# Moving the depthwise-convolution sums into PSUM, and reordering the first and the last chunk of a fused encoder block

## The chip, the cores and the metric

The kernel runs on one core of a Trainium2 chip. The metric is the device time of one execution in microseconds; lower is better. The time before is the median of three executions.

## The reference

One hybrid residual block over a sequence of 2048 positions with 1024 features, in fp32. Cut to what matters:

```python
u = rms_norm(h, g_pre_mix)
z = u @ w_in                                   # [GLU a, b | q | k | v | gates A, B]
c = a * sigmoid(b)
c = causal_depthwise_conv(c, conv_dw_w, conv_dw_b)          # 31 taps, 512 channels
y_conv = silu(layer_norm(c, conv_ln_g, conv_ln_b)) @ w_conv_out
y_attn = sliding_window_sink_attention(rope(q), rope(k), v, sinks) @ w_attn_out
h = h + rms_norm((sigmoid(gA) * y_conv + sigmoid(gB) * y_attn) @ w_out, g_post_mix)

gate, val = split(rms_norm(h, g_pre_ffn) @ w_up)            # 2 x 2816
gate = causal_depthwise_conv(gate, ffn_dw_w, ffn_dw_b)      # 3 taps
h = h + rms_norm((gelu(gate) * val) @ w_down, g_post_ffn)
h = h + (p @ w_ple) * sigmoid(h @ w_ple_gate)
```

## The kernel before

The sequence is cut into four chunks of 512 positions. Inside a chunk every activation lies feature-major: tiles of 128 features by 512 positions. Every fp32 product is made of three single-pass matmuls (`w_hi*x_hi`, `w_hi*x_lo`, `w_lo*x_hi`, lines 748 to 750, or 772, 773 and 776 where several output tiles advance together), so all activations that feed TensorE are split into a rounded part (ScalarE writes it) and the rest (VectorE subtracts).

**The weights** come as 122 blocks of eight 128x128 tiles, 512 KB each, through three slots, in the order that `block_order` writes out. In chunk 0 each block is fresh: SyncE loads it into `w_stage`, GpSimd casts it to `w_hi` (line 416) and subtracts four times to `w_lo` (line 419), and SyncE stores both halves to DRAM. Chunks 1 to 3 load the two stored halves and leave GpSimd idle. A slot is loaded again when TensorE has finished with its block (`block_done`). A block is 24 matmuls of 512 columns.

**The stages of a chunk on TensorE**: four GLU pairs; q, k, v; attention in four steps, each with two gate-A blocks, the transposes of the probabilities, the next scores and the product with v; the merge (eight gate-B blocks, four attention-out blocks, four convolution-out blocks, interleaved); `w_out`, between whose blocks the next chunk's input and the residual rows are transposed; the feed-forward in three groups of up blocks (8, 8 and 6 feature tiles, each a gate half and a value half) and a down product; the per-layer embedding. For chunks 1 to 3 the GLU pairs stand between `w_out` and the feed-forward of the chunk before, and q, k, v behind that feed-forward.

**The convolution** is VectorE work: `tap(j)` adds one of 31 taps of channel tile j into `conv_acc` in SBUF with one 128x512 instruction (line 1225), 124 taps a chunk. For chunk 0, `EARLY` = 15 taps of tiles 0 and 1 are made before `glu(0, 2)`, 15 taps of tiles 2 and 3 between the rotations (`rope`), and the remaining 64 in the four attention steps, 16 in each; then come `ln_sum`, `ln_centre`, the LayerNorm and only then the merge. For later chunks the taps stand among the up tiles of the chunk before, six to a tile and 40 in a row (`taps(40)`) beside the first down product. The mean of the LayerNorm is a matmul with ones (line 928), the token sums are matmuls with one column (line 785), and the inverse roots are spread over partitions by a matmul with a diagonal (line 792) into PSUM bank 7 (`BC`); bank 6 (`SMALL`) takes the sums.

All synchronisation is written by hand: each engine runs its own list in order and waits on counters such as `glu_done`, `merged`, `y2_out`, `v_out`, `ft_ready`. TensorE waits for `y2_out` of `w_out` tile 1 (line 1038) ahead of each of the last four `w_out` blocks. ScalarE makes `attend_q(0, 0)`, which waits for all rotations, ahead of `value_out(0)`. In the last chunk, which has no next GLU to run in between, the two norms around the residual (POST and PRE) stand one behind the other (lines 1064 to 1067) ahead of the first up blocks.

## Time and profile before

| | |
|---|---|
| median of 3 executions | 3052.34 us (3048.07 to 3063.79) |
| the profiled execution's own time | 3061.3 us |
| its span on the profile | 3059.5 us |
| mean granted TensorE clock | 0.976 |
| TensorE busy (matmuls) | 2885.7 us, 94% |
| VectorE busy | 1424.3 us, 47% |
| ScalarE busy | 805.5 us, 26% |
| GpSimd busy | 581.3 us, 19% |
| chain that ended last | TensorE 81%, VectorE 9%, GpSimd 4%, DMA 3% |

Each execution of the profile has start times counted from the beginning of its span. A busy TensorE is a matmul in flight, not TensorE at its peak; the clock column (1.00 is 2.4 GHz, 0.50 is 1.2 GHz) says how fast it was allowed to run. The chunks are told apart on TensorE's timeline by the operands: the first scores of chunk 0 start at 143.8 us and those of chunks 1, 2 and 3 at 951.9, 1668.4 and 2382.9 us.

### The profile page before, as it was taken

The page shows a single profiled execution, that of the slowest core. Times are in us where ns is not written, and L with a number is a line of the kernel's source. Part 1 is how long each engine was busy: PE and PEld are TensorE (multiplying, and loading weights), DVE is VectorE, ACT ScalarE, POOL GpSimd, SP SyncE. Part 2 cuts the span into 40 slices and gives each one's busy share as a digit, 9 for nine tenths or more (in the row PEclk, how much of TensorE's full clock was granted, in tenths as well). Part 3 has the DMA queues.
Part 4 walks back from the last instruction along what each step waited for, and adds up shares of the span by engine and source line. Part 5 has one row for each costly group of instructions (what it writes and reads, how often), then busy time and mean ns, then how long its engine had stood idle before and what let it go on. Part 6 is the DMA issues. An engine that isn't in the chain of part 4 may idle for free.

```text
span 3059.5 us, 33182 instructions
## 1 busy us (share of the span) xinstructions
PE 2885.7 (94%) x13080; PEld 2377.3 (78%) x13080; DVE 1424.3 (47%) x2392; ACT 805.5 (26%) x1539; POOL 581.3 (19%) x614
## 2 busy tenths in 40 slices
PE   6688998798999999999999999999999998899998
PEld 5576787576778888888888888888788886688886
DVE  5885359483354225674343324666325422412124
ACT  2252321111135223211224513211114512211012
POOL 5645638786643000000000000000000000000000
PEclk9799999899999999999999999999999999899999
DMA  5446857576765554555454464555455455355553
GB/s 201 169 152 246 292 205 271 184 269 232 261 223 211 203 212 176 204 193 189 173 190 179 165 240 173 197 192 195 179 186 191 159 188 190 132 194 194 189 192 138
DMA packets 182747, 606.38 MB, mean 198 GB/s; under 512 B 18752, under 2 KB 37440, under 8 KB 182592
## 3 DMA queue, kind: packets, MB, share of 16 engines
q1 hardware_dynamic: 165696, 595.86, 53.6%
q10 hardware_dynamic: 16896, 8.39, 0.9%
q8 instruction: 104, 1.70, 0.2%
q14 instruction: 51, 0.42, 0.0%
HBM read 467.87 MB, written 136.31 MB: 197 GB/s over the span
## 4 chain that ended last, share of the span: by engine, by line
PE 81%; DVE 9%; POOL 4%; DMA 3%; issue 1%; ACT 1%; SPq 0%; DVEq 0%; ACTq 0%
PE ps L748 21%; PE ps L750 21%; PE ps L749 21%; PE ps L772 4%; PE ps L773 4%; PE ps L776 4%; DVE conv_acc L1225 4%; DMA w_stage<-in_weights 3%; POOL w_lo L419 3%; POOL w_hi L416 2%; PE ps L797 1%; PE ps L885 1%; DVE h_tmp L1382 1%; DVE h L1387 1%; PE ps L792 1%
## 5 line engine op out<-in xcount | busy, mean ns | idle before, releaser
L748 PE MATMUL ps<-y_hi,w_hi 128*128 128x512 f32 x1536 | 606.1, 395 | 13.5 <-issue 6.6
L749 PE MATMUL ps<-y_lo,w_hi 128*128 128x512 f32 x1536 | 600.4, 391 | 0.0
L750 PE MATMUL ps<-y_hi,w_lo 128*128 128x512 f32 x1536 | 600.3, 391 | 0.0
L419 POOL TENSOR_TENSOR w_lo<-w_stage,w_hi 128x256 fp32r<-128x256 f32 x488 | 422.9, 897 | 9.8
L1225 DVE SCALAR_TENSOR_TENSOR conv_acc<-conv_in,col,conv_acc 128x512 f32<-128x512 f32 x480 | 396.4, 883 | 0.1
L748 PE MATMUL ps<-f_hi,w_hi 128*128 128x512 f32 x768 | 308.6, 402 | 46.1 <-POOL w_lo L419 36.7
L748 PEld LDWEIGHTS ps<-y_hi,w_hi 128*128 128x128 f32 x1536 | 289.8, 189 | 79.1 <-issue 15.7
L750 PEld LDWEIGHTS ps<-y_hi,w_lo 128*128 128x128 f32 x1536 | 289.9, 189 | 60.9
L749 PEld LDWEIGHTS ps<-y_lo,w_hi 128*128 128x128 f32 x1536 | 290.1, 189 | 59.6 <-issue 0.7
L749 PE MATMUL ps<-f_lo,w_hi 128*128 128x512 f32 x768 | 303.7, 395 | 0.0
L750 PE MATMUL ps<-f_hi,w_lo 128*128 128x512 f32 x768 | 303.0, 395 | 0.0
L748 PE MATMUL ps<-u_hi,w_hi 128*128 128x512 f32 x704 | 281.0, 399 | 3.0 <-DVE conv_in L1245 2.0
L749 PE MATMUL ps<-u_lo,w_hi 128*128 128x512 f32 x704 | 275.6, 391 | 0.0
L750 PE MATMUL ps<-u_hi,w_lo 128*128 128x512 f32 x704 | 275.6, 391 | 0.0
L1415 DVE SCALAR_TENSOR_TENSOR g_conv<-ps,col,g_conv 128x511 f32<-128x511 f32 x88 | 65.8, 748 | 364.3 <-ACT g_conv L589 364.1
L416 POOL CAST w_hi<-w_stage 128x1024 fp32r<-128x1024 f32 x122 | 159.6, 1308 | 354.2 <-DMA w_stage<-in_weights 353.9
L748 PEld LDWEIGHTS ps<-f_hi,w_hi 128*128 128x128 f32 x768 | 146.9, 191 | 87.6 <-issue 35.0
L750 PEld LDWEIGHTS ps<-f_hi,w_lo 128*128 128x128 f32 x768 | 147.0, 191 | 31.6
L749 PEld LDWEIGHTS ps<-f_lo,w_hi 128*128 128x128 f32 x768 | 147.2, 192 | 31.0 <-issue 1.0
L589 ACT ACTIVATE g_conv<-ps,col 128x512 f32<-128x512 f32 x88 | 68.5, 778 | 346.5 <-PE ps L750 284.3
L748 PEld LDWEIGHTS ps<-u_hi,w_hi 128*128 128x128 f32 x704 | 133.4, 189 | 32.9 <-issue 3.7
L1438 DVE TENSOR_TENSOR acc<-acc,ps 128x512 f32<-128x512 f32 x64 | 43.8, 686 | 245.2 <-PE ps L750 245.2
(180 smaller groups left out, 3961.2 us busy)
## 6 DMA issues: line engine op xcount, KB each, us to landing
w_hi<-split_weights SPq DMA_DIRECT2D x366, 512.0 KB, 3.2
w_lo<-split_weights SPq DMA_DIRECT2D x366, 512.0 KB, 4.2
w_stage<-in_weights SPq DMA_DIRECT2D x122, 512.0 KB, 4.5
split_weights<-w_hi SPq DMA_DIRECT2D x122, 512.0 KB, 2.8
split_weights<-w_lo SPq DMA_DIRECT2D x122, 512.0 KB, 4.0
rows_u<-in_x SPq DMA_DIRECT2D x16, 512.0 KB, 5.8
rows_h<-in_x SPq DMA_DIRECT2D x16, 512.0 KB, 6.1
out_h<-o_rows ACTq DMA_DIRECT2D x24, 256.0 KB, 2.8
```

Of the source, the lines that this page charges most:

```text
L416: nc.gpsimd.tensor_copy(w_hi[:, slot], w_stage[:, slot]).then_inc(w_hi_ready, 1)
L419: last = nc.gpsimd.tensor_tensor(w_lo[:, slot, k:k + 2], w_stage[:, slot, k:k + 2], w_hi[:, slot, k:k + 2].bitcast(F32), ALU.subtract)
L589: copy(g_conv[:, t % 2], ps[:, up_bank(t)[0]], ACT.Identity, bias=column("ffn_b", t), scale=column("ffn_w", 3 * t + 2)).then_inc(tap0_read ...
L748: nc.tensor.matmul(bank, w_hi[:, slot, kk], hi, start=start, stop=False)
L749: nc.tensor.matmul(bank, w_hi[:, slot, kk], lo, start=False, stop=False)
L750: return nc.tensor.matmul(bank, w_lo[:, slot, kk], hi, start=False, stop=stop)
L772: nc.tensor.matmul(ps[:, banks[o]], w_hi[:, slot, first + o], hi[:, k], start=(k == 0), stop=False)
L773: nc.tensor.matmul(ps[:, banks[o]], w_lo[:, slot, first + o], hi[:, k], start=False, stop=False)
L776: last = nc.tensor.matmul(ps[:, banks[o]], w_hi[:, slot, first + o], lo[:, k], start=False, stop=(k == 7))
L1225: V.scalar_tensor_tensor(dst, src, column("conv_w", t + j * TAPS), dst, ALU.mult, ALU.add).then_inc(conv_tap, 1)
L1415: V.scalar_tensor_tensor(g_conv[:, n, 1:T], gate[:, 0:T - 1], column("ffn_w", 3 * t + 1), g_conv[:, n, 1:T], ALU.mult, ALU.add).then_inc(t ...
L1438: V.tensor_tensor(acc[:, j], acc[:, j], ps[:, dn_bank(q, j)], ALU.add).then_inc(dn_acc, 1)
```

## The change

The parts, by stage:

- **Input of chunk 0.** VectorE scales two of the four row tiles and ScalarE the other two; the transposes take four PSUM banks in turn (`xu_bank`) in place of two.
- **Taps.** The running sum of `tap(j)` stands in PSUM bank 6 or 7 (`CONV_BANK`), read and written by the same instruction; one tap moves it to `conv_acc`. In chunk 0 that is tap 15 of tiles 0 and 1 and tap 7 of tiles 2 and 3, and the taps after it are in SBUF as before, because attention uses the banks. In later chunks it is the last tap, and tiles 0 and 1 are finished before tiles 2 and 3 begin.
- **Chunk 0.** 32 taps stand ahead of `glu(0, 2)`, 16 among the rotations with each rotation ahead of its four taps, nine in each attention step (36), and 40 in the merge. The merge of chunk 0 has its own block order (`FIRST_MERGE`): gate-B and attention-out blocks first, all four convolution-out blocks last. `merge_attention` puts the attention part into `h`, `merge_conv` adds the convolution part. SyncE loads the next input rows two or three blocks later. `value_out(0)` stands ahead of `attend_q(0, 0)`.
- **`w_out`.** The wait for `y2_out` moves from ahead of each block to ahead of the transposes inside it.
- **LayerNorm of the next chunk.** Its token sums and their spreading move from behind the second down product to inside up tiles 17 and 19.
- **Last chunk.** `h_split` rounds `h * g_pre_ffn`, without the inverse root, for the up product, which takes each tile as it comes. The inverse root is kept in `r_last`, and VectorE multiplies each gate and value result by it in PSUM (two more 128x512 instructions for each of the 22 tiles). The PRE sums stand behind the first two up tiles, the spreading inside the third.
- **Output of the last chunk.** Output tiles 0 to 3 are transposed between the last gate blocks in place of behind them.

```diff
+FIRST_MERGE = [b for i in range(4) for b in (GB_BLOCK[2 * i], GB_BLOCK[2 * i + 1], AT_BLOCK[i])] + CV_BLOCK
...
+        def xu_bank(c, f):
+            return 0 if c else f % 4
...
-                if c + 1 < CHUNKS and 0 <= b - (B_MRG + 9) < TT:
+                rows_with = (CV_BLOCK[2], CV_BLOCK[3], B_WO, B_WO + 1) if c == 0 else range(B_MRG + 9, B_MRG + 9 + TT)
+                if c + 1 < CHUNKS and b in rows_with:
                     sp.wait_ge(silu_ready, (c + 1) * NC)
...
+            def h_split(c, j):
+                act.wait_ge(h_mid, c * KD_ + j + 1)
+                copy(y_hi[:, j], h[:, j], ACT.Identity, bias=0.0, scale=column("g_pre_ffn", j)).then_inc(u2_hi, 1)
...
-            attend_q(0, 0)
             value_out(0)
+            attend_q(0, 0)
...
+                if c == 0:
+                    for i in range(KD_ // 2):
+                        gate_b_block(c, 2 * i)
+                        gate_b_block(c, 2 * i + 1, between=(None, None, lambda: conv_mean(0), lambda: spread(LN, 0))[i])
+                        attention_outs(c, i)
+                        if i == 2:
+                            token_sums(LN, 0)
+                    for i in range(KD_ // 2):
+                        conv_outs(c, i)
...
-                    pe.wait_ge(y2_out, c * KD_ + 2)
                     def turns(f):
+                        pe.wait_ge(y2_out, c * KD_ + 2)
...
-                    token_sums(PRE, c)
-                    spread(PRE, c)
...
+                if not more:
+                    token_sums(PRE, c)
                 for t in range(2, FB[1]):
-                    up(c, t)
+                    up(c, t, between=(lambda: spread(PRE, c)) if not more and t == 2 else None)
...
-                if more:
-                    token_sums(LN, c + 1)
...
+                    if more and t == FB[2] + 1:
+                        up(c, t, between=lambda: token_sums(LN, c + 1))
+                    elif more and t == FB[2] + 3:
+                        up(c, t, between=lambda: spread(LN, c + 1))
...
                 src = conv_in[:, j, ds(t, T)]
-                dst = conv_acc[:, j]
+                last = TAPS - 1 if conv_chunk[0] else (EARLY, EARLY, EARLY // 2, EARLY // 2)[j]
+                dst = ps[:, CONV_BANK[j % 2]] if t < last else conv_acc[:, j]
+                old = ps[:, CONV_BANK[j % 2]] if t <= last else conv_acc[:, j]
...
-                    V.scalar_tensor_tensor(dst, src, column("conv_w", t + j * TAPS), dst, ALU.mult,
+                    V.scalar_tensor_tensor(dst, src, column("conv_w", t + j * TAPS), old, ALU.mult,
                                            ALU.add).then_inc(conv_tap, 1)
...
-                    taps(6 if more else LATE)
+                    taps(4)
...
+                if c + 1 == CHUNKS:
+                    done(c, up_done(t, 0))
+                    V.tensor_tensor(gate, gate, r_last[:, :], ALU.mult).then_inc(gate_scaled, 1)
...
+                    V.tensor_tensor(val, val, r_last[:, :], ALU.mult).then_inc(val_scaled, 1)
...
                 if c == 0:
+                    taps(12)
+                    merge_attention(0)
+                    taps(14)
+                    merge_attention(1)
+                    taps(14)
                     ln_sum(0)
```

## Rows read from the trace of the kernel before

**Rows 1.** The page: busy time, share of span and instructions of each engine.

```profile
PE 2885.7 (94%) x13080; PEld 2377.3 (78%) x13080; DVE 1424.3 (47%) x2392; ACT 805.5 (26%) x1539; POOL 581.3 (19%) x614
```

**Rows 2.** Waits of TensorE, whole span: us in total, times, longest us.

```profile
PE ps L748 <- POOL w_lo L419: 43.2, 17, 22.0
PE ps L827 <- ACT v_feat L480: 25.4, 1, 25.4
PE ps L785 <- DVE ssum L1177: 23.0, 6, 15.5
PE ps L797 <- DVE rows_u L1182: 21.5, 1, 21.5
PE ps L874 <- DVE prob L1310: 8.7, 4, 4.8
```

**Rows 3.** Stages of chunks 0 and 1: busy by engine, clock, DMA share, GB/s.

```profile
143.80:227.40 83.60, 74.67 (x386) 65.06 (x385) 70.97 (x123) 44.94 (x139) 34.68 (x34) 0.87 0.40 138
227.40:331.10 103.70, 93.38 (x399) 74.34 (x399) 48.51 (x66) 22.36 (x36) 66.28 (x77) 0.97 0.69 250
331.10:951.90 620.80, 570.25 (x2472) 462.24 (x2470) 348.64 (x490) 147.51 (x230) 393.12 (x415) 0.96 0.67 243
...
951.90:1020.30 68.40, 68.40 (x417) 60.63 (x416) 27.83 (x78) 43.55 (x136) 0.00 (x0) 1.00 0.47 161
1020.30:1107.50 87.20, 87.20 (x388) 72.19 (x387) 17.45 (x28) 10.19 (x20) 0.00 (x0) 1.00 0.59 214
1107.50:1668.40 560.90, 555.38 (x2471) 456.48 (x2470) 278.07 (x490) 147.65 (x230) 0.00 (x0) 0.99 0.52 189
```

**Rows 4.** Trains of taps on VectorE's timeline: start, us, instruction.

```profile
60.93 32.18 DVE L1225 SCALAR_TENSOR_TENSOR conv_acc<-conv_in,col,conv_acc 128x512 f32<-128x512 f32 x28
...
549.41 17.97 DVE L1225 SCALAR_TENSOR_TENSOR conv_acc<-conv_in,col,conv_acc 128x512 f32<-128x512 f32 x27
```

**Rows 5.** GpSimd's timeline beside trains of taps, and just behind one.

```profile
69.34 4.50 POOL L419 TENSOR_TENSOR w_lo<-w_stage,w_hi 128x256 fp32r<-128x256 f32 x4
...
547.33 20.96 POOL L416 CAST w_hi<-w_stage 128x1024 fp32r<-128x1024 f32 x1 [9.82 <-DMA w_stage<-in_weights]
...
572.18 2.79 POOL L419 TENSOR_TENSOR w_lo<-w_stage,w_hi 128x256 fp32r<-128x256 f32 x4
```

**Rows 6.** VectorE with PSUM operands, GpSimd at work: ns min/median/max; one instruction.

```profile
L1415 DVE SCALAR_TENSOR_TENSOR g_conv<-ps,col,g_conv x8: 736/737/749, 457.0 to 522.1; 128x511 f32<-128x511 f32 x8
...
147.31 0.43 DVE L1293 TENSOR_TENSOR ps<-ps,prev_bias 128x256 f32<-128x256 f32 x1 [6.87 <-PE ps L841]
```

**Rows 7.** Start of chunk 0: ScalarE, then TensorE.

```profile
23.45 0.69 ACT L454 ACTIVATE u_hi<-ps,col 128x512 fp32r<-128x512 f32 x1 [0.17 <-PE ps L797]
...
33.19 0.80 PE L772 MATMUL ps<-u_hi,w_hi 128*128 128x512 f32 x1 [1.56 <-DVE u_lo L1186]
...
142.86 1.11 PE L827 MATMUL ps<-ident,v_feat 128*128 128x128 f32 x4 [25.44 <-ACT v_feat L480]
```

**Rows 8.** First down product of chunk 0 and 1, third up group, first up group.

```profile
530.70:600.30 69.60, 47.51 (x192) 38.45 (x193) 36.27 (x54) 4.19 (x7) 49.07 (x37) 0.83 0.47 173
...
763.40:817.80 54.40, 54.40 (x240) 44.68 (x238) 19.91 (x33) 10.09 (x15) 39.64 (x51) 1.00 0.78 289
...
1209.40:1296.70 87.30, 87.30 (x386) 72.27 (x386) 54.83 (x100) 19.71 (x29) 0.00 (x0) 1.00 0.55 202
1296.70:1340.30 43.60, 43.59 (x192) 35.77 (x191) 36.17 (x58) 4.82 (x8) 0.00 (x0) 1.00 0.53 193
```

**Rows 9.** TensorE in chunk 1: inside `w_out`, and behind the second down product.

```profile
1131.59 0.77 PE L748 MATMUL ps<-y_hi,w_hi 128*128 128x512 f32 x1 [2.20 <-issue]
...
1474.39 1.05 PE L785 MATMUL ps<-ones,ssum 128*128 128x1 f32 x8 [1.45 <-DVE ssum L1177]
```

**Rows 10.** Last chunk: from the last `w_out` block to the up blocks; the tail.

```profile
2588.40:2618.80 30.40, 7.09 (x21) 3.75 (x20) 21.80 (x47) 9.12 (x16) 0.00 (x0) 0.56 0.09 35
...
3047.60:3059.50 11.90, 4.77 (x33) 3.16 (x31) 6.44 (x10) 0.60 (x1) 0.00 (x0) 0.87 0.62 176
```

More of the change, by code:

```diff
@@ L620, in _ @@
             x_norm(0)
+            act.wait_ge(norm_step, 6)
+            for t in range(TT // 2, TT):
+                copy(rows_u[:, t], rows_u[:, t], ACT.Identity, bias=0.0, scale=n_r[:, t:t + 1]).then_inc(x_scaled, 1)
             for f in range(KD_):
@@ L728, in _ @@
                     ple_gate(c, j)
-            for f in range(KD_):
-                store_rows(CHUNKS - 1, f, o_last)
+                    if not more and j >= 5:
+                        store_rows(c, 2 * j - 10, o_last)
+                        store_rows(c, 2 * j - 9, o_last)
+            store_rows(CHUNKS - 1, 6, o_last)
+            store_rows(CHUNKS - 1, 7, o_last)
             act.wait_ge(out_stored, CHUNKS * 16 * KD_)
@@ L937, in up @@
                     full_block(c, up_block(t) + half, up_bank(t)[half], y_hi, y_lo)
+                    if half == 0 and between is not None:
+                        between()
             def down(c, q, between=None):
@@ L1119, in _ @@
                 ple_gate(c, 5)
+                if not more:
+                    out_tile(c, 0, PG_BANK[0])
+                    out_tile(c, 1, PG_BANK[1])
                 pe.wait_ge(ple_out, c * KD_ + KD_)
                 ple_gate(c, 6)
+                if not more:
+                    out_tile(c, 2, PG_BANK[0])
+                    out_tile(c, 3, PG_BANK[1])
                 pe.wait_ge(h3_step, (c + 1) * KD_)
@@ L1124, in _ @@
                 if not more:
-                    for f in range(KD_):
-                        out_tile(c, f, 6 + f % 2)
+                    for f in range(4, KD_):
+                        out_tile(c, f, PG_BANK[f % 2])
         @block.vector
@@ L1231, in taps @@
                 for _ in range(n):
-                    j = min(range(NC), key=lambda j: next_tap[j])
+                    pair = (0, 1) if conv_chunk[0] and next_tap[1] < TAPS else (2, 3) if conv_chunk[0] else range(NC)
+                    j = min(pair, key=lambda j: next_tap[j])
                     if next_tap[j] < TAPS:
@@ L1318, in attend @@
                         out_rows(c - 1, f, OT + f % 2, o_rows)
-                if c == 0 and more:
-                    taps(4)
+                if c == 0:
+                    taps(3)
                 for s in range(2):
@@ L1327, in attend @@
                                     ALU.subtract).then_inc(ao_lo, 1)
-                if c == 0 and more:
-                    taps(LATE - 10)
+                if c == 0:
+                    taps(2)
             def ln_sum(c):
@@ L1470, in _ @@
             dve.wait_ge(glu_done, 2)
-            for t in range(EARLY):
+            for t in range(EARLY + 1):
                 tap(0)
@@ L1478, in _ @@
             for j in range(PAIRS + 1):
-                for t in range(min(EARLY, 4 * j), min(EARLY, 4 * j + 4)):
-                    tap(2)
-                    tap(3)
                 if j == PAIRS:
@@ L1484, in _ @@
                 rope(0, j)
+                if j < PAIRS:
+                    for n in range(4):
+                        tap(2 + n % 2)
             for c in range(CHUNKS):
@@ L1497, in _ @@
                     ln_rest(0, 0, NC)
-                for i in range(KD_ // 2):
-                    merge(c, i)
+                    merge_attention(3)
+                    for i in range(KD_ // 2):
+                        merge_conv(i)
+                else:
+                    for i in range(KD_ // 2):
+                        merge(c, i)
                 zero_sum()
@@ L1525, in _ @@
                         residual(c, j - 1, mid_step, h_mid)
+                    if not more and j >= 1:
+                        h_rest(c, j - 1)
                     if j >= 2:
@@ L1535, in _ @@
                     glu(c + 1, 2)
+                    dve.wait_ge(bc_ready, SUM_AT[PRE, c] + 1)
+                    dve.wait_ge(h_mid, (c + 1) * KD_)
+                    for j in range(KD_ + 1):
+                        if j < KD_:
+                            u2_tile(c, j)
+                        if j >= 1:
+                            u2_rest(c, j - 1)
+                    glu(c + 1, 3)
+                    glu_keep(c + 1)
                 else:
                     zero_sum()
-                dve.wait_ge(bc_ready, SUM_AT[PRE, c] + 1)
-                dve.wait_ge(h_mid, (c + 1) * KD_)
-                for j in range(KD_ + 1):
-                    if j < KD_:
-                        u2_tile(c, j)
-                    if j >= 1:
-                        u2_rest(c, j - 1)
-                if more:
-                    glu(c + 1, 3)
-                    glu_keep(c + 1)
+                    keep_root()
                 for t in range(FB[0], FB[1]):
@@ L1573, in _ @@
                     if more and t == FB[2] + 1:
+                        token_norm(LN, c + 1, CONV)
+                        zero_sum()
+                    if more and t == FB[2] + 3:
                         ln_scale(c + 1)
@@ L1606, in _ @@
                     ple_add(c, j)
-            for f in range(KD_):
-                out_rows(CHUNKS - 1, f, 6 + f % 2, o_last)
+                    if not more:
+                        for f in (2 * j - 8, 2 * j - 7):
+                            out_rows(c, f, PG_BANK[f % 2], o_last)
             dve.wait_ge(root_ready, len(NORM_AT))
```

157 lines of the change are left out of this document (105 added, 52 removed).

## The prediction

> **What bounds the kernel now.** The page says TensorE is in flight 94% of the span [rows 1]; so the gain to be had is its idle time and its slow clock, and the question is where those lie. The list of TensorE's waits names them [rows 2]: 43 us for GpSimd's `w_lo`, one wait of 25 us for `v_feat`, 23 us for token sums (one of 15.5 us), 21.5 us at the start, 9 us for probabilities. The table of stages shows in which chunk: attention takes 83.6 us in chunk 0 and 68.4 us in chunk 1, the merge 103.7 and 87.2, and everything from `w_out` to the next scores 620.8 and 560.9 [rows 3]. Chunks 1 to 3 run at TensorE's own pace (87.2 us for 16 blocks, 5.45 us each, at clock 1.00), so nothing is won there but small waits. The loss is in chunk 0, and in the 30.4 us of the last chunk in which TensorE works 7 us [rows 10].
>
> Why chunk 0 is slow shows when VectorE's trains of taps are laid beside GpSimd's timeline. A tap costs 32.18/28 = 1.15 us while GpSimd works on weights and 17.97/27 = 0.67 us where it does not [rows 4]. GpSimd pays too: four subtractions take 4.50 us beside taps and 2.79 us without, and one cast that came in the middle of `taps(40)` took 20.96 us, until the train was over [rows 5]. That is the 22 us wait of TensorE. A tap reads two SBUF tensors. The instructions of the up tiles that read one operand from PSUM keep 736 to 749 ns while GpSimd works [rows 6]. A tap with its sum in PSUM should do the same.
>
> **The change part by part.** *Price of a tap in PSUM.* No instruction of the trace has the full form (SBUF and PSUM in, PSUM out, 512 wide). The nearest rows are the PSUM-reading one (737 ns in duration, as a free tap) and the one that reads and writes the same PSUM bank, 256 wide in 0.43 us [rows 6], which is 0.16 us plus 256 elements at 0.96 GHz, as for SBUF. So I take 0.67 us. Bounds: not below 0.6, and up to 1.15 if it still meets GpSimd. The Trainium skill, VectorE: DVE Perf Modes, section on the TRN2 errata, speaks against the change: it gives a PSUM source 62 cycles more fixed cost than an SBUF source, by its figures an estimated 65 ns a tap; over the 44 taps before the scores that would take 3 us from the gain, 2928 in place of 2925. The durations of rows 6 do not show it.
>
> *Start.* The first GLU matmul is at 33.19 us [rows 7] and the first transposes at 21.5 [rows 2]. With two of four rows scaled on ScalarE they start about 2.5 us sooner, and with four banks the eight tiles follow at 0.86 us (the start of the second rounding, 23.45, less the first 0.86 before it) in place of pairs at 2.74: 18.9 + 1.1 + 7 x 0.86 + 1.7 for the last two eviction steps = 27.7. Gain 5.5 us.
>
> *To the scores, before at 143.8.* VectorE now does 32 taps in 21.4 us after `glu(0, 1)` (before 33.7), so `glu(0, 2)` and `(0, 3)` are in time for q and k, and TensorE's eight GLU and six q, k, v blocks run through: 27.7 + 46.2 + 33.9 = 107.8. Each rotation (2.0 us) with four taps (2.7) fits in a 5.45 us block, so the key's rotation ends near 109, `value_out` no longer waits for `attend_q`, and the scores start near 110.5. The 25.4 us idle [rows 7] and the slow clock behind it go. Gain so far 33.3 us.
>
> *Attention, before 83.6.* Nine SBUF taps in a step in place of 16. Chunk 1 shows the pace without taps, 68.4 with 2 us of output transposes [rows 3]. VectorE's other work is 6.6 us a step, nine taps at 1.15 add 10.4, against a TensorE step of 16.3: just even. I take 68.3 with 2 us for jitter and clock: gain 15.3. Gate-B starts near 179.
>
> *Merge, before 103.7.* 16 blocks are 87.2 [rows 3]. What is late next is `conv_mean`, which TensorE now issues inside the eighth block, 41 us in. VectorE still has 42 SBUF taps, two pieces of attention merge and three sums: at 1.15 us it is ready some 16 us late, at 0.67 some 5 us late; in the wait GpSimd runs dry and the last taps get cheap, so 12. With 2.5 us of slow clock behind the wait, and 3 us for weights (GpSimd needs 1.5 + 4.5 = 6.0 us for a block beside taps [rows 5], more than TensorE's 5.45; SyncE's queue holds the load of the third convolution block behind `silu_ready`), this stage costs 104.7, nothing won. The moved row loads are covered: the rows are wanted 22 us into `w_out`. `w_out` starts near 283.5: gain 47.6 in all, bounds 38 and 58.
>
> *Rest of chunk 0, before 620.8.* Chunk 1's 560.9 less 6.7 us (next part) is the clean length, 554. To it comes what fresh weights cost even without taps: two blocks must be there at each down product, about 3 us and the clock three times, 6 us before the embedding and 6 us in small waits. So 575. The largest piece is the first down product, 69.6 against 43.6 us [rows 8]. The third up group (54.4 us in chunk 0, no taps beside it) shows that the fresh stream holds TensorE's pace, at 289 GB/s [rows 8]. Gain 45.8, bounds 30 and 57.
>
> *`w_out` and LayerNorm.* TensorE stands 2.2 us for `y2_out` [rows 9], and a slow-clock window behind it doubles some matmuls, another 1.4 us. Moved nine matmuls (2.0 us) further back, the wait is nearly met. The token sums wait 1.45 us [rows 9] and again cost about 1.6 in clock; two up tiles later VectorE has long summed. Gain 6.7 us in each of chunks 1 and 2 (13.4), and 2.1 for `w_out` in chunk 3; chunk 0's share is in its 575.
>
> *Last chunk.* The 30.4 us [rows 10] lose the wait for PRE. The residual tiles start at 2595.8; the first is normed, added, rounded and subtracted by 2599. Then each tile costs VectorE 2.5 us and 0.7 us of waiting for ScalarE's rounding, 3.2, against 2.72 for TensorE's 12 matmuls: the first up product ends near 2622.5 in place of 2642.6. Token sums, spreading, and a stall of 0.7 us at up tile 3, which waits for the first scaled tile, take back 2.8. Gain 17.3, bounds 12 and 20. The 44 scalings are 0.68 us each, hidden: a tile has 10.9 us on TensorE and its chain through VectorE and ScalarE is under 7. Tail: four output tiles earlier, but 2.2 us of their transposes now stand ahead of the last gate: gain 0.7 of 11.9 [rows 10].
>
> **Sum**: 47.6 + 45.8 + 13.4 + 2.1 + 17.3 + 0.7 = 126.9. The profiled execution's own time is 3061.3 (span 3059.5), so 2934.4; the median of the runs is 9.0 below it: 2925.
>
> **The rivals.** *A: the taps in PSUM still collide with GpSimd.* The source is still in SBUF. Against it stand rows 6, of just such mixed operands. Then 32 taps take 36.8 us before `glu(0, 2)`, each rotation step exceeds a block, and the cast can starve: some 15 us of the opening and 35 of the rest are lost, 2975.
>
> *B: the fresh weights bind.* Faster consumption asks for a block every 5.45 us all through chunk 0; a load takes some 5 us and GpSimd 3.9 to 6.0, with only two blocks of cover (10.9). For it: 43 us of waits for `w_lo` now. Against it: the third up group. If half of the FFN gain goes (23) and the merge loses 9 more: 2957.
>
> *C: slower than before.* An instruction that reads and writes one bank at full width might run far slower than the half-wide one of the trace [rows 6]. The first up group of chunk 1 has VectorE busy 54.8 of 87.3 us with 42 taps [rows 8], so a tap can grow by 0.77 us, to 1.44, unseen. There are 252 such taps in three chunks; to eat 127 us each must cost 0.5 more: from about 1.95 us a tap the kernel is slower than before, at 2.0 it takes some 3066.
>
> *D: a long starved cast in the merge.* Trains of 12 and 14 SBUF taps remain; a cast that meets one waits up to 9 us, most of it inside the wait already counted. 2932, within the forecast's own range.
>
> **How the numbers follow.** The forecast 0.74 (with D), A 0.07, B 0.15, C 0.02, and 0.02 for an effect under 15 us. Its own range is the sum of bounds, 2903 to 2952. To leave out no more than 2 in 10 the range reaches to B: 2900 to 2965. What a measurement of this kernel can tell is about 0.5%, 15 us: faster 0.95, same 0.03, slower 0.02.
>
> **What would show it.** In the profile after: taps into PSUM at 0.67 us beside a working GpSimd; no cast over 2 us in the feed-forward; scores of chunk 0 near 110; one wait of TensorE of some 12 us at the mean of the LayerNorm, near 220; the first down product of chunk 0 under 50 us; chunks 1 and 2 at about 710 us each; less than 12 us between the last residual transposes and the first up matmul of chunk 3. It is wrong if waits for `w_lo` stay near 40 us (B), if taps in PSUM take over 0.8 us (A, C), or if VectorE in attention is late and the steps stay near 19 us.

## The result: 3.5% faster, and what the trace after shows

The changed kernel takes 2949.68 us (median of 4 runs, 2943.44 to 2954.17), against 3057.35 us for the kernel before on the same chip (4 runs, 3048.07 to 3063.79). The ratio is 0.9646, 95% interval 0.9625 to 0.9666: 107.7 us less. The forecast was 2925 with a range from 2900 to 2965. The two profiled executions are 3061.3 and 2943.4, 117.9 apart, where the sum of the prediction said 126.9.

The page of the changed kernel, busy time of each engine (answers to [rows 1]):

```profile
PE 2854.6 (97%) x13080; PEld 2358.7 (80%) x13080; DVE 1405.2 (48%) x2427; ACT 807.6 (27%) x1541; POOL 523.2 (18%) x614
```

TensorE has the same 13080 matmuls, but is 31 us less in flight with them: fewer ran at the lower clock (the mean granted clock is 0.991, before 0.976). GpSimd has the same 614 instructions in 523.2 us in place of 581.3, although no edit touches them.

The changed kernel's waits of TensorE (answers to [rows 2]): us in total, times, longest us.

```profile
PE ps L828 <- DVE rows_u L1236: 19.1, 1, 19.1
PE ps L779 <- POOL w_lo L433: 14.1, 10, 2.4
PE ps L964 <- DVE ssum L1397: 13.6, 1, 13.6
```

The 43.2 us for `w_lo` are 14.1, no wait for them is over 2.4 us, and the waits for `v_feat` and `prob` have left the head of the list. One wait has grown, that of the mean of chunk 0's LayerNorm for the channel sum: 13.6 us, where the same matmul stood 7.5 us in the kernel before:

```profile
PE ps L928 <- DVE ssum L1334: 7.5, 1, 7.5
```

The changed kernel by stages (answers to [rows 3], [rows 8] and [rows 10]). Columns: stretch, us, busy time of PE, PEld, DVE, ACT, POOL, granted clock, DMA share, GB/s. They are chunk 0's attention, its merge, the rest up to the next scores; the first down product of chunk 0; chunk 1 whole; the last chunk from its last residual transposes to the first up matmul; its first up product; the last chunk from its scores.

```profile
107.70:176.60 68.90, 68.61 (x385) 60.18 (x385) 51.58 (x101) 45.54 (x141) 34.85 (x39) 0.95 0.53 183
176.60:286.70 110.10, 94.19 (x398) 74.69 (x396) 87.47 (x101) 21.83 (x35) 79.18 (x77) 0.92 0.64 234
286.70:865.20 578.50, 558.18 (x2471) 456.30 (x2472) 314.49 (x490) 148.41 (x231) 342.40 (x415) 0.99 0.72 261
...
478.00:526.10 48.10, 45.97 (x193) 37.23 (x194) 37.55 (x57) 4.19 (x7) 30.25 (x38) 0.96 0.68 256
865.20:1575.50 710.30, 707.58 (x3272) 587.06 (x3271) 324.38 (x596) 201.34 (x385) 0.00 (x0) 1.00 0.53 191
2489.20:2499.50 10.30, 3.17 (x12) 1.52 (x11) 5.25 (x16) 4.00 (x7) 0.00 (x0) 0.75 0.28 102
2499.50:2525.10 25.60, 25.07 (x99) 19.88 (x99) 18.95 (x29) 9.07 (x15) 0.00 (x0) 0.90 0.39 131
2285.80:2941.60 655.80, 635.49 (x2919) 524.50 (x2917) 229.03 (x432) 153.56 (x312) 0.00 (x0) 0.99 0.50 181
```

Set against [rows 3], these lines say where the time came from. Scores of chunk 0 start at 107.7 in place of 143.8: 36.1 us. Attention is 14.7 us shorter, the merge 6.4 us longer, the rest of chunk 0 42.3 us shorter (the down product of [rows 8], 69.6, is 48.1). Chunk 1 gives 6.2 and chunk 2 4.2; the last chunk the remainder, in which the 30.4 us of [rows 10] are 10.3. So 87 of the 118 us lie in chunk 0; some 6 of them are the earlier start (experiment 5), and most of the others lie behind taps and weights (experiments 2 and 3).

The changed kernel's taps on VectorE by form, both beside GpSimd for a part of the time: us busy, mean ns of one.

```profile
L1286 DVE SCALAR_TENSOR_TENSOR ps<-conv_in,col,ps 128x512 f32<-128x512 f32 x388 | 267.1, 748 | 0.0
...
L1286 DVE SCALAR_TENSOR_TENSOR conv_acc<-conv_in,col,conv_acc 128x512 f32<-128x512 f32 x76 | 78.2, 1094 | 0.1
```

A tap with its sum in PSUM lasts 748 ns (its duration; one follows the other every 0.67 us), and its spread over the whole kernel is 739 to 756 ns. Of the 388 taps, 97 have GpSimd at work for over 80% of their time and 256 have it idle; the median is 749 ns in both groups, so GpSimd's work does not reach them. The 76 taps of chunk 0 that kept their sum in SBUF last 1094 ns on average. It is the second operand read from SBUF that costs, not the sum written there: the four taps before the scores that read the sum from PSUM and write it to SBUF, with GpSimd at work beside them for most of their time, last 740 to 748 ns.

### The profile page after: what moved, and what is told of

Its sections match the earlier page's. It is cut to its first block, busy times and chain, and to the rows that moved or that the text cites. A ratio compares the mean times of both kernels' runs of the same rounds, so it can differ in the third digit from the quotient of the medians.

```text
span 2941.6 us, 33211 instructions
## 1 busy us (share of the span) xinstructions
PE 2854.6 (97%) x13080; PEld 2358.7 (80%) x13080; DVE 1405.2 (48%) x2427; ACT 807.6 (27%) x1541; POOL 523.2 (18%) x614
## 4 chain that ended last, share of the span: by engine, by line
PE 87%; DVE 7%; DMA 2%; POOL 2%; ACT 1%; issue 1%; SPq 0%; DVEq 0%; ACTq 0%
PE ps L779 23%; PE ps L781 23%; PE ps L780 23%; PE ps L803 4%; PE ps L804 4%; PE ps L807 4%; DVE conv_acc L1286 2%; DMA w_stage<-in_weights 2%; PE ps L828 1%; POOL w_lo L433 1%; PE ps L917 1%; DVE h_tmp L1467 1%; DVE h L1472 1%; DVE y_lo L1551 1%; PE ps L876 1%
## 5 line engine op out<-in xcount | busy, mean ns | idle before, releaser
L779 PE MATMUL ps<-y_hi,w_hi 128*128 128x512 f32 x1536 | 603.2, 393 | 1.7 <-POOL w_lo L433 1.7
L433 POOL TENSOR_TENSOR w_lo<-w_stage,w_hi 128x256 fp32r<-128x256 f32 x488 | 388.6, 827 | 9.8
L1286 DVE SCALAR_TENSOR_TENSOR ps<-conv_in,col,ps 128x512 f32<-128x512 f32 x388 | 267.1, 748 | 0.0
L430 POOL CAST w_hi<-w_stage 128x1024 fp32r<-128x1024 f32 x122 | 135.1, 1107 | 325.8 <-DMA w_stage<-in_weights 325.7
L803 PE MATMUL ps<-y_hi,w_hi 128*128 128x512 f32 x384 | 152.5, 397 | 9.3 <-ACT ple_last L633 4.1
```

The source lines that it names most:

```text
L430: nc.gpsimd.tensor_copy(w_hi[:, slot], w_stage[:, slot]).then_inc(w_hi_ready, 1)
L433: last = nc.gpsimd.tensor_tensor(w_lo[:, slot, k:k + 2], w_stage[:, slot, k:k + 2], w_hi[:, slot, k:k + 2].bitcast(F32), ALU.subtract)
L779: nc.tensor.matmul(bank, w_hi[:, slot, kk], hi, start=start, stop=False)
L803: nc.tensor.matmul(ps[:, banks[o]], w_hi[:, slot, first + o], hi[:, k], start=(k == 0), stop=False)
L1286: V.scalar_tensor_tensor(dst, src, column("conv_w", t + j * TAPS), old, ALU.mult, ALU.add).then_inc(conv_tap, 1)
```

## The experiments

All times are medians. Ratios are to the kernel before, with 95% intervals; differences between variants are between their medians. The variants were timed in four sets, in which the kernel before had 3054.7 to 3057.0 us, so such a difference is good to some 3 or 4 us. They are taken against the 2947.66 us of experiment 1.

**1. Both kernels again.** The changed kernel again, unedited:

> The changed kernel once more, unaltered, as the yardstick for the others. Theory: 0.9646 of the time before, about 2950 us; its profile again has the first scores of chunk 0 near 107.7 us, a wait of some 13.6 us for the three sums ahead of the mean, and no cast on GpSimd over 2 us. Rival (part of the gain is luck of one execution): a ratio over 0.972.

2947.66 us, 0.9644 (0.9630 to 0.9658). Its profile has the scores of chunk 0 at 108.1, attention 68.7, merge 109.8, rest of chunk 0 581.1.

The kernel before again, unedited, one execution:

> The kernel before once more, for a second trace. Theory: the long cast on GpSimd beside the 40 taps comes in each execution of this kernel, since the same instructions meet, and the opening stages keep their lengths within 2 us. Rival: whether a cast starves depends on the execution; then its trace has no cast over 2 us or has it elsewhere, and its time differs by up to 15 us.

3055.55 us. The stages before `w_out` repeat within 0.6 us (scores at 143.6, attention 83.3, merge 103.1), the rest of chunk 0 is 5 us shorter (615.9), and the same cast of the weights is long again: 21.1 us, after 20.96 in [rows 5]. TensorE's waits for `w_lo` are 41.4 us in 16 waits, the longest 22.0. The starved cast belongs to the program's order and is no accident of one execution.

**2. The orders without the PSUM sums.** All sums of the convolution in SBUF again, everything else as changed:

```diff
-                dst = ps[:, CONV_BANK[j % 2]] if t < last else conv_acc[:, j]
-                old = ps[:, CONV_BANK[j % 2]] if t <= last else conv_acc[:, j]
+                dst = old = conv_acc[:, j]
```

> The changed kernel with every tap's sum in SBUF again, all orders kept. Theory (the PSUM sums keep VectorE off GpSimd's way, and this carries a large part of the gain): taps beside GpSimd cost 1.15 us again, the scores of chunk 0 start some 15 us later, the rest of chunk 0 is some 30 us longer, total near 2995 us. Rival (the new orders make the gain, the place of the sum hardly matters): under 2960 us.

2992.52 us, 0.9790 (0.9777 to 0.9804): 44.9 us over the changed kernel, as expected. TensorE's waits in this variant:

```profile
PE ps L779 <- POOL w_lo L433: 32.7, 19, 8.8
...
PE ps L871 <- ACT q_diag L512: 10.8, 1, 10.8
```

The weights are late again, the scores start at 124.9, and the rest of chunk 0 is 609.0. GpSimd's timeline and VectorE's of the same variant, beside the train of taps in chunk 0's first down product: start, us, instruction, and idle time before it.

```profile
518.28 6.83 POOL L430 CAST w_hi<-w_stage 128x1024 fp32r<-128x1024 f32 x1 [11.17 <-DMA w_stage<-in_weights]
```

```profile
510.87 13.34 DVE L1285 SCALAR_TENSOR_TENSOR conv_acc<-conv_in,col,conv_acc 128x512 f32<-128x512 f32 x20
524.12 2.12 DVE L1281 TENSOR_SCALAR conv_acc<-conv_in,col 128x512 f32<-128x512 f32 x2
526.17 4.91 DVE L1285 SCALAR_TENSOR_TENSOR conv_acc<-conv_in,col,conv_acc 128x512 f32<-128x512 f32 x4
```

The reader is to see three things. The cast begins inside the train of 20 taps, which goes on at 0.67 us a tap as if nobody else were there. The cast ends at 525.1, a microsecond after the train's end at 524.1, when the first taps of the other pair (one SBUF operand, L1281) were issued. From then on both sides pay: four taps take 4.91 us, 1.23 each. So this cast was held for the rest of the train, and got in where another kind of instruction followed. Here the pair order ended the train after 20 taps, and the cast took 6.8 us, not 21.

**3. The PSUM sums without the orders.** The kernel before, with only the sums moved, and pairs of channels as the change has them in chunks 1 to 3:

```diff
+                last = TAPS - 1 if conv_chunk[0] else EARLY - 1
+                dst = ps[:, CONV_BANK[j % 2]] if t < last else conv_acc[:, j]
+                old = ps[:, CONV_BANK[j % 2]] if t <= last else conv_acc[:, j]
```

> The kernel before with only the taps' sums moved to PSUM (in chunk 0 the first 14 taps of each tile, in the other chunks 30 of 31), all orders as before. Theory: rotations and taps before the scores are about 25 us shorter, the feed-forward of chunk 0 about 40 us, total near 2990 us. Rival (without the new order the taps are not what TensorE waits for): no better than 3030 us.

2999.02 us, 0.9815 (0.9799 to 0.9832): 57.4 us less than before. TensorE's waits in this variant:

```profile
PE ps L749 <- POOL w_lo L420: 16.0, 8, 3.7
...
PE ps L828 <- ACT v_feat L481: 9.2, 1, 9.2
```

Of the 43.2 us for `w_lo` [rows 2] 16.0 are left and of the 25.4 for `v_feat` 9.2, with every order as it was, but for the pairs of channels among the taps of the next chunk (which experiment 2 has too, with 32.7 us of waits for `w_lo`). The scores start at 122.6 (21 us earlier, 25 expected), the rest of chunk 0 is 587.4 (33 us shorter, 40 expected); attention, whose taps keep their sums in SBUF, is 82.2 (before 83.6 and 83.3), and chunk 1 is 716.1, as before. Rival A (taps in PSUM still collide) falls.

**4. What ends the hold.** Twice the kernel before, with nothing moved. First, in trains of eight taps and more, one short instruction stands after every fourth tap; it writes a zero into an unused column and reads nothing:

```diff
                     if next_tap[j] < TAPS:
                         tap(j)
+                        if n >= 8 and tapped[0] % 4 == 0:
+                            V.memset(breath[:, breaths[0]:breaths[0] + 1], 0.0)
+                            breaths[0] += 1
```

> The kernel before with one more instruction of VectorE after every fourth tap in the trains of 8 taps and more: it fills one unused column with zero, and reads nothing from SBUF. Theory (a GpSimd cast that meets a train of taps is held until something else than a tap is issued): the long cast of 21 us shrinks to some 5 us, the wait of TensorE for the low parts of the weights in chunk 0 falls from 22 us to under 10, w_out to the next scores takes about 605 in place of 616 to 621, and the time falls by 8 to 14 us (ratio 0.995 to 0.998). Rival: the cast needs a longer pause than one short instruction, or only its own luck: it takes 15 us or more again and the time is the same (ratio 0.999 to 1.002).

3045.67 us, 0.9960 (0.9947 to 0.9973). More work, and 10.7 us less time. GpSimd and then VectorE at the place of [rows 4, 5], in this variant:

```profile
544.12 1.59 POOL L417 CAST w_hi<-w_stage 128x1024 fp32r<-128x1024 f32 x1 [11.47 <-DMA w_stage<-in_weights]
545.79 4.44 POOL L420 TENSOR_TENSOR w_lo<-w_stage,w_hi 128x256 fp32r<-128x256 f32 x4
```

```profile
541.41 2.74 DVE L1226 SCALAR_TENSOR_TENSOR conv_acc<-conv_in,col,conv_acc 128x512 f32<-128x512 f32 x4
543.43 0.06 DVE L1239 MEMSET breath<- 128x1 f32 x1
544.07 4.45 DVE L1226 SCALAR_TENSOR_TENSOR conv_acc<-conv_in,col,conv_acc 128x512 f32<-128x512 f32 x4
```

The next tap starts 0.58 us after the end of the 0.06 us instruction, so each of them opens the train. The cast, which took 20.96 us, takes 1.59; no cast of the kernel is over 1.62 us. It came 0.05 us after a restart, so that it was never held; that an opening frees one that is held is not seen here. The longest wait of TensorE for `w_lo` falls from 22.0 to 5.5 us, their sum from 43.2 to 26.0, and the rest of chunk 0 from 620.8 to 604.2. What stays is the price of sharing: taps of 1.1 us and subtractions of 4.44.

So, second, one opening only, placed behind the moment at which the cast is asked for:

```diff
-                    taps(40)
+                    taps(22)
+                    V.memset(breath[:, c:c + 1], 0.0)
+                    taps(18)
```

> The kernel before with one more short instruction (a zero into an unused column) after the 22nd of the 40 taps of each train in the feed-forward, and nowhere else. In the trace of before the train of chunk 0 starts at 540.8 and runs at 0.67 us a tap, and the cast is asked for at 547.33, 6.5 us into it, and held to the end. Theory (a held cast gets in at the first opening, whatever its time): the opening comes at 540.8 + 22 x 0.67 = 555.5, the cast ends near 556.6 and takes 9 to 10.5 us, the 18 taps behind it share at 1.1 to 1.2 us each, the longest wait of TensorE for the low parts of the weights falls from 22 to about 11 us, and the time falls by 7 to 12 us (ratio 0.996 to 0.998). Rival (one short opening does not help a cast that is already held; in the kernel with an opening every four taps it only was asked for beside one): the cast takes 21 us again, the wait stays at 22, ratio 0.999 to 1.001.

3047.87 us (11 runs) against 3054.73 (15 runs), 0.9982 (0.9973 to 0.9991): the gain is real, but some 6 us (3 to 8 by the interval) where 7 to 12 were expected. GpSimd and VectorE in this variant:

```profile
545.37 10.03 POOL L417 CAST w_hi<-w_stage 128x1024 fp32r<-128x1024 f32 x1 [9.62 <-DMA w_stage<-in_weights]
555.48 4.43 POOL L420 TENSOR_TENSOR w_lo<-w_stage,w_hi 128x256 fp32r<-128x256 f32 x4
```

```profile
554.45 0.06 DVE L1555 MEMSET breath<- 128x1 f32 x1
555.87 19.86 DVE L1226 SCALAR_TENSOR_TENSOR conv_acc<-conv_in,col,conv_acc 128x512 f32<-128x512 f32 x17
```

The cast is asked for 5.5 us into the train, stands through it, and ends at 555.40, 0.9 us after the one opening at 554.45: 10.03 us where 9 to 10.5 were expected. The 17 taps that follow take 19.86 us, 1.17 each, and TensorE's longest wait for `w_lo` is 12.8 us in place of 22.0. The rival, that an opening does not help a held cast, falls. Only some 6 us of the 9 come out at the end. The likely reason, not tested by itself, is that the blocks behind the cast now share with the rest of the train, 4.4 us for their subtractions each; with the sums in PSUM they don't.

**5. The parts of the change undone singly.** The merge of chunk 0 in the old order, so that all 76 SBUF taps stand in its attention:

```diff
-        order += [(c, b) for b in (FIRST_MERGE if c == 0 else range(B_MRG, B_WO))]
+        order += [(c, b) for b in range(B_MRG, B_WO)]
...
+                gate_b_block(c, 0)
+                gate_b_block(c, 1, between=(lambda: conv_mean(0)) if c == 0 else None)
+                attention_outs(c, 0)
```

> The changed kernel with the merge of chunk 0 in its old order (block order, input row loads, convolution-out blocks among the others) and all 76 taps that are left after the rotations in the four attention steps, 19 in each. The taps before the scores stay in PSUM. Theory (spreading 40 taps over the merge is worth what attention gained, since the stage's own length did not fall): attention is about 20 us longer, the merge about 8 us shorter, total some 10 us over the changed kernel, near 2960 us. Rival (reordering only moved the wait): within 4 us of the changed kernel.

2963.24 us, 0.9693 (0.9679 to 0.9707), 15.6 more than the changed kernel. Attention grows by 23 us to 91.6 and the merge shrinks by 9.7 to 100.5. The new merge order thus pays in the stage ahead of it, by what it lets attention leave undone.

The last chunk in the old order (normed h before the first up product):

```diff
                     for j in range(KD_):
-                        h_split(c, j)
                         mid_square(c, j)
                     sum_root(PRE, c, D)
+                    for j in range(KD_):
+                        u2_tile(c, j)
```

> The changed kernel with the last chunk normalised as before: POST and PRE one behind the other ahead of the up blocks, no scaling of gate and value in PSUM. Theory: 17 us more, near 2966 us, all of it between the last residual transposes and the end of the first up product. Rival (the start on unnormalised tiles is given back later, since VectorE now sets the pace of that product and has 44 more instructions): under 8 us more.

2965.18 us, 0.9705 (0.9691 to 0.9718), 17.5 more; from `w_out` to the end the last chunk takes 517.6 in place of 500.2.

The wait for `y2_out` and the token sums of the next LayerNorm where they were:

```diff
+                    pe.wait_ge(y2_out, c * KD_ + 2)
+
                     def turns(f):
-                        pe.wait_ge(y2_out, c * KD_ + 2)
...
+                if more:
+                    token_sums(LN, c + 1)
                 turn_p(c)
```

> The changed kernel with the wait for the two evicted tiles of the out projection ahead of each block again, and the LayerNorm sums of the next chunk behind the second down product again. Theory: 3.5 us in each of four chunks and 3 in each of three less what chunk 0 hides, 15 to 20 us more in all, near 2967 us; the wait of 2.20 us and the slow clock behind it are back. Rival (other work takes up the slack): under 6 us more.

2965.55 us, 0.9702 (0.9687 to 0.9717), 17.9 more: chunks 1 and 2 are 716.1 and 714.6 again in place of 710.3 each, and the rest of chunk 0 is 587.3 in place of 578.5 and 581.1.

The start of chunk 0 as before (rows scaled on VectorE alone, two banks for the transposes):

```diff
-            return 0 if c else f % 4
+            return 0 if c else 2 * (f % 2)
...
-                for t in range(TT if c else TT // 2):
+                for t in range(TT):
```

> The changed kernel with the start of chunk 0 as before: all four rows are scaled on VectorE, and the first transposes go through two banks in pairs. Theory: the first GLU matmul comes at about 33.2 us in place of 27.0, all later stages keep their lengths, and the time is 6 us above the changed kernel (ratio to the kernel before 0.966 to 0.967). Rival: the 6 us are given back, because the first weights or the taps set the time of the scores: then the scores of chunk 0 stay near 108 and the time at 0.9646.

2953.82 us, 0.9665 (0.9653 to 0.9678), 6.2 more. Its profile shows the scores of chunk 0 at 115.8, 8.1 later than in the changed kernel, and all later stages within 3 us of it. So nothing hides the start; by the medians it is worth the 5.5 us of the forecast, a little more.

**6. A faster kernel: the last taps too.** The wait for the channel sum is the largest new one. Its chain is 40 SBUF taps, and the two banks are free again once the attention is out. The last 40 taps of chunk 0 go there as well:

```diff
+                again = t >= LAST_TAPS and not conv_chunk[0]
-                dst = ps[:, CONV_BANK[j % 2]] if t < last else conv_acc[:, j]
-                old = ps[:, CONV_BANK[j % 2]] if t <= last else conv_acc[:, j]
+                dst = ps[:, CONV_BANK[j % 2]] if t < last or again and t < TAPS - 1 else conv_acc[:, j]
+                old = ps[:, CONV_BANK[j % 2]] if t <= last or again and t > LAST_TAPS else conv_acc[:, j]
```

> The changed kernel, and the last 40 taps of chunk 0, which stand in the merge, also sum in PSUM: banks 6 and 7 are free again behind the attention. 36 of the 40 then cost 0.67 us in place of about 1.15. Theory (the wait of 13.6 us ahead of the mean is the price of SBUF taps beside GpSimd): the wait nearly goes, with the slow clock behind it: 15 us less than the changed kernel, near 2935 us, a ratio to before near 0.960. Rival (the merge is held by fresh weights or by the place of the attention merges among the taps): under 5 us less.

2937.05 us, 0.9608 (0.9595 to 0.9621): 10.6 less than the changed kernel, where 15 were expected. VectorE's timeline in this variant:

```profile
202.25 2.72 DVE L1293 SCALAR_TENSOR_TENSOR ps<-conv_in,col,ps 128x512 f32<-128x512 f32 x4
209.76 1.29 DVE L1457 TENSOR_TENSOR h<-ps,gate_b 128x512 f32<-128x512 f32 x2 [4.79 <-PE ps L782]
210.96 7.99 DVE L1293 SCALAR_TENSOR_TENSOR ps<-conv_in,col,ps 128x512 f32<-128x512 f32 x12
```

The taps are now so fast that the third lot stands behind a piece of the attention merge that TensorE has not made yet: 4.79 us idle, then the lot, and TensorE waits 5.48 us for the sum that follows. The miss is this: a wait in VectorE's order, that the slow taps had covered. The prediction's merge paragraph had already priced it ("at 0.67 some 5 us late"); the expectation of this variant left it out. The edit that follows from the line:

```diff
-                    taps(12)
-                    merge_attention(0)
-                    taps(14)
-                    merge_attention(1)
-                    taps(14)
+                    taps(20)
+                    merge_attention(0)
+                    taps(20)
+                    merge_attention(1)
```

> The kernel with the last taps of chunk 0 in PSUM too, and these 40 taps in two lots in place of three (20, the first piece of the attention merge, 20, the second piece, and the channel sum at once). In the three-lot kernel VectorE stood 4.79 us for the second attention block before its last lot, and TensorE 5.48 us at the mean. Theory: the lot no longer stands behind that wait, the channel sum comes some 4 us sooner, the mean wait is under 2 us, the merge takes about 94 us in place of 99.9, and the time is about 2931, 0.958 to 0.959 of the kernel before. Rival: the second piece of the merge comes 2 us later than now and holds its bank, so that the third attention block waits, or weights bind: no change against 2937 (0.9608).

2930.74 us, 0.9591 (0.9579 to 0.9604), 6.3 less again; the four times of either variant don't overlap. The merge is 91.4 us; TensorE has no wait left at the mean, and in the whole merge 0.8 us for `w_lo`. This is the fastest version: 4.1% under the kernel before.

## Why the prediction was right, and where its sizes were off

**Start and scores: right.** First GLU matmul at 26.99 (27.7 said), scores of chunk 0 at 107.7 (110.5 said). The rotation of the key kept up, and the queue of q, k, v blocks ran through.

**Price of a tap in PSUM: right.** 0.67 us was said and 0.67 is the pace; the longest of 388 is 756 ns. The durations of the nearest rows, 736 to 749 [rows 6], were the right bound. An SBUF tap in a free train has the same 0.67 us pace [rows 4] and lasts 745 ns. The Trainium skill (VectorE: DVE Perf Modes, TRN2 errata) gives a PSUM source 62 cycles more than an SBUF source, by its figures an estimated 65 ns a tap. No such difference is to be seen here. So rivals A and C did not come. C's threshold was too high besides: its 252 taps leave out the 120 that stand 40 in a row, where VectorE has only 43.6 - 36.2 = 7.4 us to spare [rows 8]. With them the kernel would have been slower than before from some 1.6 us a tap (an estimate), not 1.95.

**Attention: right** (68.9, said 68.3).

**Merge: mis-sized, 110.1 where 104.7 was said.** The mechanism was in the main as described: the sum is late, and TensorE waits. Its lines in the changed kernel:

```profile
218.70 0.39 PE L781 MATMUL ps<-u_hi,w_lo 128*128 128x512 f32 x1
232.66 2.07 PE L964 MATMUL ps<-ssum,ones 128*128 128x512 f32 x2 [13.57 <-DVE ssum L1397]
233.75 1.41 PE L779 MATMUL ps<-u_hi,w_hi 128*128 128x512 f32 x1
234.96 0.63 PE L780 MATMUL ps<-u_lo,w_hi 128*128 128x512 f32 x1
```

The wait is 13.6 (12 said). One step of the working did not come: that GpSimd runs dry in the wait and the last taps get cheap. VectorE's timeline has the last lot of the changed kernel at 1.05 us a tap; GpSimd was at work beside it until 228.6, all but its last 1.9 us:

```profile
198.15 16.49 DVE L1286 SCALAR_TENSOR_TENSOR conv_acc<-conv_in,col,conv_acc 128x512 f32<-128x512 f32 x14
214.57 1.27 DVE L1449 TENSOR_TENSOR h<-ps,gate_b 128x512 f32<-128x512 f32 x2
215.77 14.66 DVE L1286 SCALAR_TENSOR_TENSOR conv_acc<-conv_in,col,conv_acc 128x512 f32<-128x512 f32 x14
```

Weights cost 1.6 (3 said). The term that was missing shows in the last variant, which has no wait at the mean and a full clock: 91.4 us, 0.8 of them for weights, against the 87.2 of 16 blocks. The other 3.4 us come with the mean, the token sums and the spreading, which stand among the blocks of chunk 0 only; their twelve matmuls fill 1.7 us by themselves, and why the stage pays double was not taken apart. The sum of the prediction did not have them. The clock cost what was said. Behind the wait a matmul takes 0.63 us in place of 0.39, as the lines above show, until the clock comes back at 238.2:

```profile
232.60:238.20 5.60, 5.54 (x11) 3.72 (x12) 2.98 (x6) 0.00 (x0) 0.00 (x0) 0.50 0.01 3
```

That is 5.6 us at the lower level (1.2 GHz), for work of half that time: 2.8 us (2.5 said). Left are 110.1 - 87.2 - 13.6 - 1.6 - 3.4 - 2.8 = 1.5 us; 0.8 of them are an idle time of TensorE ahead of the first `w_out` matmul, behind which the profile shows no wait and which the last variant does not have, and 0.7 stay open. The differences, +1.6, -1.4, +3.4, +0.3 and +1.5, are the 5.4 us. Rival D, a cast held for 9 us, did not come: no cast of this kernel came after more than 2.3 us of taps running alone, and the longest cast of the kernel is 1.52 us.

**Rest of chunk 0: right within 4 to 6** (578.5, said 575; 581.1 in the second profile). Waits for `w_lo` are 13.2 us of it, and with the merge's 14.8 in all, where the kernel before has 43.2: rival B did not come. Five of them, 10.9 us together, lie in the down products, two in the first, two in the second and one in the third, and in the first two the second wait comes 19 us after the first; TensorE's lines of the changed kernel:

```profile
477.98 0.47 PE L779 MATMUL ps<-f_hi,w_hi 128*128 128x512 f32 x1 [2.18 <-POOL w_lo L433]
497.01 0.47 PE L779 MATMUL ps<-f_hi,w_hi 128*128 128x512 f32 x1 [2.13 <-POOL w_lo L433]
...
615.35 0.47 PE L779 MATMUL ps<-f_hi,w_hi 128*128 128x512 f32 x1 [2.20 <-POOL w_lo L433]
...
634.40 0.47 PE L779 MATMUL ps<-f_hi,w_hi 128*128 128x512 f32 x1 [1.94 <-POOL w_lo L433]
...
734.35 0.47 PE L779 MATMUL ps<-f_hi,w_hi 128*128 128x512 f32 x1 [2.41 <-POOL w_lo L433]
```

The prediction put them down to the two blocks that a down product wants at its start. For the waits 19 us into a down product that can't be the reason; no variant with another order of the down product was run, and what spaces these blocks stays open.

**Chunks 1 and 2: 10.4 where 13.4 was said.** The two waits are gone, as the undoing of this part shows. The prediction missed two things. First, a new wait: with the token sums moved away, the transposes of p stand directly behind the second down product and wait for its last evictions. In chunk 1 of the changed kernel:

```profile
PE ps L828 <- DVE acc L1541: 0.9, 1, 0.9
```

In the kernel before only the last chunk, which had no such sums, had this wait. Second, the clock behind the waits. In the kernel before, these are the stretches after the second down product in chunks 1 and 2:

```profile
1470.00:1485.00 15.00, 13.55 (x61) 11.07 (x61) 5.20 (x14) 2.89 (x5) 0.00 (x0) 0.89 0.33 115
...
2186.00:2200.00 14.00, 12.55 (x64) 10.39 (x63) 5.69 (x16) 3.34 (x5) 0.00 (x0) 1.00 0.38 140
```

The wait is the same 1.45 us in both, but the clock fell only in chunk 1 (0.89 against 1.00). The prediction took chunk 1's row for both, at 1.6 us each. In the second profile of the kernel before it is the other way round: behind the same wait the clock is 1.00 in chunk 1, and 0.91 over 20 us in chunk 2.

**Last chunk: right.** Gap 10.3 (under 12 said), the first product ends at 2525.1, 35.9 us after the residual transposes (34.1 said). By the undone variant this part gives 17.4 us, and 17.3 was said. The whole chunk is 20.8 us shorter; the other 3.4 are `w_out` and the tail, for which 2.8 were said.

**From the profile to the median: the weakest step.** "9.0 below the profile" came from a median of three runs. With more runs the kernel before stands at 3056, 5 below its profile, and the profile of the changed kernel is at the low end of its runs, 6 below their median. Of the 24 us by which 2925.4 was too low, 9 are the sum (126.9 against 117.9) and 15 are this step. Both errors point the same way, and the time lies only 2 us inside the prediction's own range, 2903 to 2952. (The bounds that it lists add up to 2901 to 2956.) The wider range, to 2965, was stretched for rival B, which did not come; that the time is well inside it says little for the sum.

**The whole by parts.** PSUM sums alone give 57.4 us, the orders alone 63.9 (the kernel before at 3056.4 against 2992.5), both 107.7 to 108.8: 12 to 14 us are won by either. The held cast is likely a piece of that: 20.96 us before, 6.8 with the new orders alone, and none over 1.64 with the PSUM sums alone. Undone singly, the parts cost 44.9 (PSUM), 17.9 (small waits), 17.5 (last chunk), 15.6 (merge order) and 6.2 (start), together 102. Such costs need not add up to the whole, since some of the time is won by either of two parts. The orders ahead of the scores and the tail were undone by no run.

## What to carry to other kernels

When two engines share SBUF, look at the neighbour's instructions too: the taps themselves took 0.67 or 1.15 us, but the longest single wait, 22 us, was for a weight cast beside them, held until the train was over. An accumulator that one engine updates in place, and that fits in a free PSUM bank, belongs there; where it can't go, a train of such instructions is better broken every few steps (0.4% here). And after each gain read the wait list and the order of the queue again: a wait that a slow instruction had covered (4.79 us in the first late variant) comes out as soon as the instruction is fast.

## What the hardware showed

**A held cast.** A GpSimd cast of 128x1024 takes 1.04 us alone. Four casts of these traces came late into a gapless train of taps in SBUF and were held to its end or its first opening: 20.96 and 21.1 us beside 40 taps (asked for 6.5 and 6.4 us into the train), 6.8 us beside 20 (7.4 us in), 10.03 us with one opening (5.5 us in). All four stand at the same place of the program, chunk 0's first down product. The taps keep 0.67 us meanwhile. What sets the held casts apart is not how far into the train they came: others came up to 26 us into one and took 1.6 us or less, but GpSimd had paused for 2.7 us at most before those. It is how long the taps had run alone, with GpSimd idle, just before the cast. Of the casts in all traces that met a train of four taps and more, those with up to 3.0 us of taps alone before them took 1.0 to 1.6 us, and the four with 5.5 us and more were held. Where between 3.0 and 5.5 us the one turns into the other, and why, no run here shows.

The Trainium skill (SBUF — State Buffer, SBUF: two separate sides) has an exclusive lock between the two engines, which the first to start gets for the whole instruction, while the other fully blocks. The traces agree that a held cast stands; they do not agree on the length, since it lost to all instructions left in the train, up to 30 taps, and not to one.

**Sharing in turn.** When GpSimd was at work from the start of a train, both were slower: taps 1.05 to 1.23 us, casts 1.50, four subtractions 4.50 against 2.79. Beside taps with their sum in PSUM a cast takes 1.04 us, as alone.

**One SBUF operand is not always enough.** `TENSOR_SCALAR` on one 128x512 tile in SBUF (line 1207 of the kernel before) takes 0.43 us with GpSimd idle and 0.84 us beside its subtractions. What the taps gained is shown for their own form only, a `SCALAR_TENSOR_TENSOR` with one operand in PSUM.

**A sum in PSUM at the SBUF pace.** Reading and writing the same bank at full width costs 748 ns, against 745 for the SBUF form in a free train; the pace is 0.66 us in both.

**The clock.** The same wait of 1.45 us is followed by a granted clock of 0.89 in one chunk and of 1.00 in the next, and in another execution of the same kernel it is the other way round. What decides it, no run here shows.
